# Token order of the weight products in a two-layer fp32 kernel: from 256 tokens in sequence to runs of 16 that alternate between the two halves of the row

## The reference

```python
proj = rms_norm(x, norm1_w) @ w_in            # 2048 x 5648
x = x + concatenate([attn, ssm]) @ w_out      # 2048 x 2048
u = causal_dwconv(rms_norm(x, norm2_w) @ w_up, ...)   # 2048 x 11264
x = x + (silu(u_gate) * u_val) @ w_down       # 5632 x 2048
mod = silu(c) @ w_ada + b_ada                 # one row only
proj = einsum('bsd,df->bsf', h, w_in_2)       # 2048 x 7168
out = einsum('bsf,fd->bsd', y, w_out_2)       # 2048 x 2048
```

## Time and profile before

| | |
|---|---|
| median of 2 executions | 1540.61 us (1540.24 to 1540.98) |
| profiled execution, first to last instruction (span) | 1537.5 us |
| TensorE matmuls busy / weight loads busy | 1524.5 / 1483.7 us |
| VectorE / ScalarE busy | 1136.1 / 778.1 us |
| HBM, mean over the span | 220 GB/s |

### The profile page before, as it was taken

How to read it: one execution, slowest core, us unless ns; L and a number is a source line. 1 busy time by engine, 2 the same in 40 slices (tenths; PEclk the granted TensorE clock), 3 DMA queues, 4 the chain that set the end, 5 groups by cost and what they waited for, 6 DMA issues and landing times. The chain is left out here.

```text
span 1537.5 us, 32072 instructions
## 1 busy us (share of the span) xinstructions
PE 1524.5 (99%) x12586; PEld 1483.7 (97%) x12586; DVE 1136.1 (74%) x1373; ACT 778.1 (51%) x930; POOL 29.8 (2%) x56
## 2 busy tenths in 40 slices
PE   9999999999999999999999999999999999999997
PEld 8999997999999999999999999999999989999997
DVE  7877777657987878788788887879854644764754
ACT  7645455545554444444444444445554643454554
POOL 0000000000000000000000000000000000000000
PEclk9999999999999999999999999999999999999999
DMA  9474556457877767677686776866465554445451
GB/s 348 171 272 161 200 177 220 146 171 273 302 282 249 288 233 273 244 249 274 235 293 229 262 272 221 300 219 217 150 247 194 196 193 162 160 159 185 154 186 58
DMA packets 85932, 339.23 MB, mean 221 GB/s; under 512 B 9680, under 2 KB 10208, under 8 KB 79328
## 3 DMA queue, kind: packets, MB, share of 16 engines
q1 hardware_dynamic: 77760, 281.05, 52.1%
q0 software_dynamic: 7232, 54.55, 10.1%
q10 hardware_dynamic: 864, 2.53, 0.4%
HBM read 335.97 MB, written 2.12 MB: 220 GB/s over the span
## 5 line engine op out<-in xcount | busy, mean ns | idle before, releaser
L683 DVE TENSOR_TENSOR wlo<-raw,whi 128x1024 fp32r<-128x1024 f32 x528 | 643.3, 1223 | 345.9 <-ACT whi L320 342.2
L320 ACT ACTIVATE whi<-raw 128x1024 fp32r<-128x1024 f32 x528 | 557.5, 1059 | 646.5 <-PE PS L1328 573.6
L1324 PE MATMUL PS<-gh,whi 128*128 128x256 f32 x3096 | 863.7, 279 | 0.7 <-DVE gl L1208 0.3
L1326 PE MATMUL PS<-gl,whi 128*128 128x256 f32 x3096 | 856.1, 277 | 0.0
L1328 PE MATMUL PS<-gh,wlo 128*128 128x256 f32 x3096 | 856.1, 277 | 0.0
L1324 PEld LDWEIGHTS PS<-gh,whi 128*128 128x128 f32 x3096 | 581.7, 188 | 5.9 <-issue 2.6
L1326 PEld LDWEIGHTS PS<-gl,whi 128*128 128x128 f32 x3096 | 581.4, 188 | 0.8
L1328 PEld LDWEIGHTS PS<-gh,wlo 128*128 128x128 f32 x3096 | 581.6, 188 | 0.0
L1324 PE MATMUL PS<-ah,whi 128*128 128x256 f32 x688 | 189.9, 276 | 0.0
L1328 PE MATMUL PS<-ah,wlo 128*128 128x256 f32 x688 | 189.9, 276 | 0.0
L1326 PE MATMUL PS<-al,whi 128*128 128x256 f32 x688 | 189.9, 276 | 0.0
(11 more groups left out here) (256 smaller groups left out, 894.6 us busy)
## 6 DMA issues: line engine op xcount, KB each, us to landing
raw<-weights SPq DMA_DIRECT2D x528, 512.0 KB, 3.6
ada_w<-w_ada POOLq DMA_DIRECT2D x48, 1024.0 KB, 5.9
EM<-rows POOLq DMA_DIRECT2D x1, 3072.0 KB, 12.4
X<-xT SPq DMA_DIRECT2D x3, 512.0 KB, 8.3
c<-const ACTq DMA_DIRECT2D x1, 1536.0 KB, 7.1
c_act<-c_rows POOLq DMA_DIRECT2D x1, 1024.0 KB, 7.0
outT<-X SPq DMA_DIRECT2D x2, 512.0 KB, 3.2
outT<-X SPq DMA_DIRECT2D x3, 256.0 KB, 2.2
```

Of the source, the lines that this page charges most:

```text
L320: act.activation(whi[:, j % SPLIT, :], raw[:, j, :], ACT.Copy).then_inc(s_hi, 1)
L683: dve.tensor_tensor(wlo[:, j % SPLIT, :], raw[:, j, :], whi[:, j % SPLIT, :].bitcast(F32), ALU.subtract).then_inc(s_lo, 1)
L1324: pe.matmul(out[:, t, :], whi[:, b, w], hi[:, kt, :], start=first and half == 0 and (apart or t % 2 == 0), stop=False, skip_group_check=True)
L1326: pe.matmul(out[:, t, :], whi[:, b, w], lo[:, kt, :], start=False, stop=False, skip_group_check=True)
```

## The change

In `product` alone, the 256 tokens that move, and the 256 sums that are written, are taken in another order. `runs` views the row as 2 halves x 8 x 16 and walks it as tokens 0-15, 128-143, 16-31, 144-159, and so on to 112-127, 240-255. Source and destination have the same order, so each sum lands where it did. Number, size and order of the instructions, the waits and the values are unchanged; the weights are loaded as before.

```diff
+            def runs(row):
+
+                return row.rearrange("p (h c i) -> p c h i", h=2, i=16)
+
             def product(b, out, tiles, first, last, hi, lo, apart=False, ready=None):
...
-                        pe.matmul(out[:, t, :], whi[:, b, w], hi[:, kt, :], start=first and half == 0 and (apart or t % 2 == 0),
+                        pe.matmul(runs(out[:, t, :]), whi[:, b, w], runs(hi[:, kt, :]), start=first and half == 0 and (apart or t % 2 == 0),
                                   stop=False, skip_group_check=True)
-                        pe.matmul(out[:, t, :], whi[:, b, w], lo[:, kt, :], start=False, stop=False,
+                        pe.matmul(runs(out[:, t, :]), whi[:, b, w], runs(lo[:, kt, :]), start=False, stop=False,
                                   skip_group_check=True)
-                        mm = pe.matmul(out[:, t, :], wlo[:, b, w], hi[:, kt, :], start=False, stop=last and half == 1,
+                        mm = pe.matmul(runs(out[:, t, :]), wlo[:, b, w], runs(hi[:, kt, :]), start=False, stop=last and half == 1,
                                        skip_group_check=True)
```

## The result

The changed kernel takes 1608.67 us (1608.58 to 1608.77) against 1540.61: slower by 4.4%, ratio 1.0443 (95% interval 1.0427 to 1.0460). The forecast was 1518.

A forecast was written before the change was run, and what follows sets the result against it. TensorE alone was taken to bound the kernel, by matmul count times start distance. Savings of 11,352 x 1.6 ns = 18.2 us and 4.3 us turn 1537.5 into 1515.0; 3.1 us from span to median give 1518.1 us, range 1486 to 1590.

The forecast's parts named there:

- The second form at 117.8 ns: Stretches with the same instructions but longer start distance: some 950 matmuls, costing 4.3 us in all.
- step 1: Token read in `product`: walking in step with the weight load should end collisions; best 109 ns, worst 117.8 per matmul.
- The argument from pace: Token read in `product`: within 512 bytes it walks at the load's pace, so the starting distance, 192 or 448, stays.
- The worst case of step 1: Token read in `product`: all matmuls take the longer form, 117.8 ns.
- Step 2: Weight load behind each `product` matmul: sets a floor of 111.7 ns, so the win is 1.6 ns, not 6.6.
- Step 3: PSUM writes in 64-byte pieces: taken as 0, upper bound 6.7 ns per matmul.
- Step 4: Splits and DMA behind TensorE: nothing new is late; VectorE at most a few us at the peak of `w_ada`.
- D: Rival, all 11,352 `product` matmuls: bad fixed distance or a cost per piece, 1587.5 or 1616.7 us; chance 0.28.
- fixed bad distance: Token read and weight load in `product`: in step they stay at one distance and, if bad, collide all the way.
- first price: All `product` matmuls at 117.8 ns: 47 us more, 1587.5 us.
- The second: A whole column time for each of 16 pieces in every `product` matmul: 76 us more, 1616.7 us.
- The remark against D: Places 192 and 448 are 64 short of a multiple of 256, so the token read follows one piece behind the load.

The follow-up runs named there:

- weights_moved: Kernel before the change with the weights whi and wlo 64 bytes further on and the tokens where they were: 1605.29 us.
- both_moved: Kernel before the change with weights and tokens both 64 bytes further on: 1539.03 us.
- write_runs_only: Changed kernel with the tokens read in sequence again and only the sums written in runs of 16: 1540.27 us, ratio 1.0000.
- short_load: Changed kernel, feed-forward up groups loading 32 of 128 weight columns; first group in runs of 16, second in sequence: 119.9 and 116.7 ns per matmul.
- runs_of_64: Changed kernel with runs of 64 tokens instead of 16, everywhere: 1540.51 us, ratio 1.0001.
- fixed_load: Changed kernel, feed-forward up groups loading one weight column 128 times; first group in runs of 16, second in sequence: 120.0 and 116.7 ns per matmul.

## Why the prediction was wrong

The steps on what bounds the kernel held: TensorE alone, and the number of matmuls by the distance of their starts. That the operands' standing to each other moves this distance held too: `weights_moved` and `both_moved` show it. The second form at 117.8 ns isn't explained by that, since it occurs at the place 192 as well (and `write_runs_only` from 20 to 33 us).

What failed is step 1 of the change, "if collisions between the two reads are what is lost, they should go". It took the whole loss for meetings of two walks, and so made reads in step the best case; the sum has 111.7 ns where 120.0 were measured. Point by point:
- Reading in runs of 16 costs 3.3 ns more than the sequence with hardly a load beside it (`short_load`, 116.7 and 120.0). Step 1 had no term for this; only the rivals did.
- Beside a full load at the places 192 and 448 the sequence loses 6.6 ns, not 10. It had been at its best already, and breaking it every 64 bytes loses that: the other 3.3 ns of the 6.7. This split sets one measured difference beside another; no run changes the one part and keeps the other. Among the orders only 256 bytes in one piece kept 113.3.
- The argument from pace ("both walk at the same pace") is refuted by the orders with 15 breaks at three paces, 120.0 to 121.4 ns, and by runs of 8 at the same pace, 123.4.
- The worst case of step 1, "the longer form, 117.8, for all", was no upper bound: 120.0 lies above it.

Step 2 (a load floor of 111.7) was never reached, so it is untested. Step 3, writes at 0, was right to 0.12% (`write_runs_only`). Step 4 held: VectorE's wait for ScalarE only grew.

Of the rivals D, with its chance at 0.28, was right in sign and place. Of its two mechanisms the fixed bad distance isn't borne out: with `gh` and `gl` moved to 64 the runs still take 120.0. The other ("each of the 16 pieces costs something on the read or write side") holds on the read side, in direction. Its first price, 117.8 for all, was too small by 2.2 ns. The second, a column time per piece, gives 1616.7 us against 1608.7, and that it comes so near is luck: 8 pieces lose 5.5 ns over the sequence and not 3.3, and 4 pieces lose nothing. The range ended at 1590, just above the first price, and so missed; it left out the upper bound that step 3 had worked out itself. The remark against D, that 192 and 448 would put the token read one piece behind the load, was a guess with no row behind it.

The rule of the Trainium skill (PSUM — Partial Sum Buffer, Specifications) that any access that isn't contiguous slows matmuls significantly does not hold here for writes in pieces of 64 bytes (`write_runs_only`, ratio 1.0000). The Trainium skill (Advanced Engine Details and Errata, PSUM Cachelines) repeats that rule and adds that every two neighbours should be contiguous for best throughput; pieces of 64 bytes fulfil this second one, and `write_runs_only` agrees with it.

Left open: why 192 beyond a multiple of 256 is good for the sequence, what makes a stretch there take 117.8 ns instead of 113.3, and what the 120.0 consists of. In column times at 2.4 GHz the three steady values 113.3, 116.7 and 120.0 ns are 272, 280 and 288, the 256 columns and 16, 24 and 32 more; no run tells what these steps of 8 are. No version faster than both kernels came out; the best, `runs_of_64` and `both_moved`, equal the kernel before.

## What to carry to other kernels

In a stream of fp32r matmuls with 256 moving columns and a fresh 128-column load each, read the distance between starts, not busy time, and compare it with the bare columns: here 6.6 ns of 113.3 are overhead, and at other places it was up to 13.3. In this kernel the moving operand had to stay in pieces of 256 bytes, while the output could be in pieces of 64. Try the distance between the moving and the loaded operand first: 64 bytes of padding were worth 65 us here. When an order of access is tried, measure read side and write side apart, and the read beside a short load, before building a reason on the two together.

## What the runs showed of the hardware

- With a load of 32 columns, or of 128 equal ones, beside it, an fp32r matmul of 256 columns takes 116.7 ns in sequence and 120.0 in runs of 16: 10 and 13.3 over the bare columns (`short_load`, `fixed_load`).
- With a full load beside it the same sequence was faster (113.3 at the place 192) or slower (120.0 at 128, 64 bytes off, in `weights_moved`).
- Moving weights and tokens together by 64 bytes changed nothing (`both_moved`, 113.3 ns).
- At one and the same place, 192, stretches of the sequence take 113.3 or 117.8 ns (kernel before).
- Output in pieces of 64 bytes: ratio 1.0000 (0.9988 to 1.0011).
- Reading and writing 8 of every 16 bytes at a time doubles the time of a matmul, 229.3 ns.
